# The products of the five lower decay levels: one product of a whole chunk against four quarter products

## The chip, the cores and the metric

The kernel runs on one core of one Trainium2 chip. The metric is the device time of one execution in microseconds (us); the median of three runs before is 3709.82 us (3709.05 to 3710.29).

## The reference, cut to what matters

The program is a stack of one block (a hybrid mixer and a mixture of experts) and two layers of a second block. The second block has four mixing branches. Two of them, the HGRN-2 branch and the gated linear attention (GLA) branch, decay their state by channel: within a chunk the score of query t and key s is a sum over channels d in which each channel has its own decay.

```python
cum = jnp.cumsum(fc, axis=-2)
rel = jnp.where(causal, cum[..., :, None, :] - cum[..., None, :, :], -jnp.inf)
scores = jnp.einsum('bhtd,bhsd,bhtsd->bhts', qc, kc, jnp.exp(rel))
o = jnp.einsum('bhts,bhsv->bhtv', scores, vc) + jnp.einsum('bhtd,bhdv->bhtv', qc * jnp.exp(cum), state)
```

## The kernel before, in words

The 1024 tokens are taken as 8 chunks of 128. A "unit" is a head, or a pair of heads. Each of the two layers runs 12 units in the order `KIND = "ssgghhhhrrrr"`: two SSM units, two GLA units (`g`, two heads of 64 channels each, which lie on partitions 0 to 63 and 64 to 127), four HGRN units (`h`, one head of 128 channels), four retention units. Only `g` and `h` decay by channel. So there are 4 units of kind `g` and 8 of kind `h` in the program.

For these the 128 by 128 square of scores of a chunk (keys down, queries across) is built by levels (`tensor_decay`, lines 1726 to 1787). Level l, of 0 to 6, has half width h = 2^l. It cuts the 128 tokens of a chunk into blocks of 2h tokens; in each block the keys are the first h tokens and the queries the last h. `vector_decays`, `scalar_decays` and `vector_factors` write for each level one tile E with both: the keys times their decay to the middle of the block stand in the first h columns of a block, the queries times theirs in the last h. TensorE multiplies the two, and VectorE's `copy_predicated` (line 1825) puts the result into the tile P of scores, under a mask `lm` that is true only where key and query lie in the same block (line 1822 and `constants()`). The mask drops everything else that a product has computed, or left from earlier, in its bank of PSUM.

In levels 0 to 4 the kernel before issues one product for each chunk and head: its fixed operand (the weights that are loaded into the array) is the whole chunk, 128 columns, and its moving operand is all 64 query columns of the level. In levels 5 and 6 it issues one product for each block (two of 32 columns fixed and 32 moving; one of 64 and 64). The operands are f32. In the trace each f32 product has two weight loads and two matmuls.

The order of the work is written out by hand. Each engine runs the program of a unit (its "core", here `tensor_decay`, `vector_decay`, `scalar_decay`) interleaved with the preparation of the next unit (`prep`: the projections on TensorE, lines 136 to 138, in three rounded products each; the split of their weights on ScalarE line 1357 and VectorE line 1362; conv, gates and cumulative sums). `PACE` says how many steps of the preparation stand ahead of each step of the core, the same for all engines (line 3830). On VectorE the step of level l holds `copy_predicated` of level l, the differences of level l + 3 (lines 1664, 1666), the factors of level l + 2 (lines 1683, 1687), then steps of the preparation. On TensorE it is the products of the level and then projections. An `h` unit with an even number prepares an odd one, which has no projection of values, so that it has few steps of preparation; an odd one prepares an even one (or the first retention unit). After level 6 TensorE waits for the decayed keys (`kfac_last`, VectorE line 1838), which it transposes (line 1525).

Of the kernel before, what the change touches and what calls it, by code (L numbers as in the profile page):

```python
# [67 lines left out]
class Marks:  # L68
# [5 lines left out]
    def up(self, signal, *key, by=1):  # L74
        name = HOME.get(signal, signal)
        n = self.n[name] = self.n.get(name, 0) + by
        assert not self.dry or (signal,) + key not in self.place
        self.place[(signal,) + key] = n
        return self.sem.get(name), by

    def at(self, signal, *key):
        if self.dry:
            return None, 1
        return self.sem[HOME.get(signal, signal)], self.place[(signal,) + key]
# [42 lines left out]
def c8(t):  # L127
    return t.rearrange("p (c t) -> p c t", t=128)
# [31 lines left out]
def build(nc, d, out):  # L160
    ctx = ExitStack()
    with ctx:
# [43 lines left out]
        def tl(*key):  # L206
            i = wa.has[key]
            return WA[:, i * 1024:(i + 1) * 1024]
# [5 lines left out]
        def ps(*key):  # L214
            return bank_aps[banks.has[key]]

        def free(e, room, *key):
            for end in room.was[key]:
                e.wait_ge(*at(*end))
# [1081 lines left out]
        def count(U):  # L1301
            return 2 if KIND[U % 12] == "g" else 1
# [7 lines left out]
        def k_ready(U):  # L1310
            kind = KIND[U % 12]
            return ("rot", U, 1) if kind == "r" else ("copied", "k", U, 1) if kind == "g" else ("kscaled", U) if U >= 12 else ("ksig", U)

        def head_rows(U, n):

            return slice(n * 64, (n + 1) * 64) if KIND[U % 12] == "g" else slice(0, 128)
# [203 lines left out]
        def tensor_turn(t, U, src, ready):  # L1520
            t.wait_ge(*at(*ready))
            for i in range(2):
                free(t, banks, "turn", U, i)
                for j in range(4):
                    o = t.transpose(ps("turn", U, i)[:, j * 128:(j + 1) * 128], c8(src)[:, 4 * i + j, :], ident)  # L1525
                o.then_inc(*up("turn", U, i))
# [13 lines left out]
        def tensor_states(t, U):  # L1540
            t.wait_ge(*at("copied", "v", owner(U), 3))
            for i in range(2):
                free(t, banks, "kv", U, i)
                t.wait_ge(*at("turned", U, i))
                for c in range(4 * i, min(4 * i + 4, 7)):
                    for n in range(count(U)):
                        rows = head_rows(U, n)
                        o = t.matmul(ps("kv", U, i)[rows, (c % 4) * 128:(c % 4) * 128 + 128], c8(tl("KE", U))[:, c, rows], val(U, n, c),  # L1548
                                     start=True, stop=True)
                o.then_inc(*up("kv_mm", U, i))  # L1550
# [21 lines left out]
        def tensor_outputs(t, U, n, qd, masked):  # L1572
            P, s, rows = tl("P", U, n), tl("s", U), head_rows(U, n)
            t.wait_ge(*at(*masked(1)))
            for i in range(2):
                free(t, banks, "o", U, n, i)
                for j in range(4):
                    c = 4 * i + j
                    t.matmul(ps("o", U, n, i)[:, j * 128:(j + 1) * 128], val(U, n, c), c8(P)[:, c, :], start=j == 0, stop=False)  # L1579
            for i in range(2):  # L1580
                t.wait_ge(*at("state", U, 3 + 3 * i))
                for j in range(4):
                    c = 4 * i + j
                    if c:
                        o = t.matmul(ps("o", U, n, i)[:, j * 128:(j + 1) * 128], c8(s)[rows, c, :], c8(qd)[rows, c, :], start=False,  # L1585
                                     stop=j == 3)
                o.then_inc(*up("o_mm", U, n, i))
# [13 lines left out]
        def tensor_norm(t, U, n):  # L1601
            for i in range(2):
                free(t, banks, "om", U, n, i)
                t.wait_ge(*at("osq", U, n, i))
                t.matmul(ps("om", U, n, i), ones, half(tl("osq", U, n), i), start=True, stop=True).then_inc(*up("om_mm", U, n, i))  # L1605
# [126 lines left out]
        def tensor_decay(t, U):  # L1732
            N = range(count(U))
            q, k = tl("q", U), tl("k", U)
            t.wait_ge(*at("copied", "q", U, 1))
            t.wait_ge(*at(*k_ready(U)))
            for i in range(2):
                for n in N:
                    free(t, banks, "base", U, n, i)
                for j in range(4):  # L1740
                    c = 4 * i + j
                    for n in N:
                        rows = head_rows(U, n)
                        o = t.matmul(ps("base", U, n, i)[:, j * 128:(j + 1) * 128], c8(k)[rows, c, :], c8(q)[rows, c, :],  # L1744
                                     start=True, stop=True)
                        if j == 3:
                            o.then_inc(*up("scores", U, n, i))

            def products(l):
                h = 1 << l  # L1750
                E = tl("E", U, l)
                t.wait_ge(*at("fac", U, l))
                for n in N:
                    free(t, banks, "pd", U, l, n)
                for c in range(8):
                    for n in N:
                        rows = head_rows(U, n)
                        chunk = c8(E)[rows, c, :]
                        if l < 5:
                            second = chunk.rearrange("p (j b) -> p j b", b=2 * h)[:, :, h:2 * h]  # L1760
                            o = t.matmul(ps("pd", U, l, n)[:, c * 64:(c + 1) * 64].rearrange("p (j r) -> p j r", r=h),  # L1761
                                         chunk if l else c8(k)[rows, c, :], second, start=True, stop=True)
                        for b in range(0, 128 if l >= 5 else 0, 2 * h):
                            o = t.matmul(ps("pd", U, l, n)[b:b + h, c * 64 + b // 2:c * 64 + b // 2 + h], chunk[:, b:b + h],
                                         chunk[:, b + h:b + 2 * h], start=True, stop=True)
                        if c == 7:
                            o.then_inc(*up("prod", U, l, n))

            for l in range(6):
                yield  # L1770
                products(l)
            yield
            products(6)
            tensor_turn(t, U, tl("F", U), ("kfac_last", U))
            yield
            tensor_states(t, U)
            yield
            t.wait_ge(*at("qfac_last", U))
            for n in N:
                tensor_outputs(t, U, n, tl("E", U, 7), lambda i: ("placed", U, 6, n))  # L1780
                yield
                tensor_norm(t, U, n)
# [2643 lines left out]
```

## Time and profile before

| | before |
|---|---|
| median of 3 runs | 3709.82 us |
| the profiled execution | 3709.18 us, of which the span from first to last instruction is 3707.4 us |
| PE busy | 3526.8 us (95%) |
| DVE busy | 1964.9 us (53%) |
| ACT busy | 1572.8 us (42%) |
| mean granted TensorE clock | 0.976 |

PE is TensorE's matmul row, PEld its weight loads, DVE VectorE, ACT ScalarE. A busy PE counts each matmul from its start to its modelled end, and matmuls overlap, so a busy share says little on how dense the work is; the starts in a timeline do. A granted clock of 1.00 is 2.4 GHz, 0.50 is 1.2 GHz. The levels lie in two parts of the span: 1811 to 2222 us (layer 0: units 2 and 3 of kind `g`, then 4 to 7 of kind `h`) and 2895 to 3320 us (layer 1, units 14 to 19).

### The profile page before, as it was taken

The numbers are of one execution on the slowest core, as the hardware profiler recorded it, in microseconds if no ns is written. First come the engines' busy times: TensorE is split into PE (matmuls) and PEld (weight loads), VectorE is DVE, ScalarE is ACT, GpSimd is POOL, SyncE is SP. The second block draws the span as 40 slices with busy tenths as digits, with TensorE's granted clock in tenths as the row PEclk, the third lists the DMA queues.
The fourth block names the chain that finished last, engine by engine and source line by source line (L and its number), as shares of the span: only waits on it lengthen the run. The fifth ranks groups of instructions, "written<-read, shape, count | busy, mean of one in ns | idle before, by whom it ended". The sixth has DMA issues, their size and how long they took to land.

```text
span 3707.4 us, 45567 instructions
## 1 busy us (share of the span) xinstructions
PE 3526.8 (95%) x18870; PEld 2833.7 (76%) x18870; DVE 1964.9 (53%) x2556; ACT 1572.8 (42%) x1826; POOL 90.9 (2%) x90
## 2 busy tenths in 40 slices
PE   7999999989999997999999999999999999999998
PEld 5787667766666664778887888787778887888777
DVE  4544443465555554655555563445565556663434
ACT  4322101355545552543346454434443456653433
POOL 0000000000000002000000000000000000000000
PEclk9999999989999998999999999999999999999999
DMA  5101342369999996122111011243122101011332
GB/s 199 46 26 52 125 155 90 127 248 369 370 367 373 367 366 254 64 69 80 46 46 58 21 66 58 76 179 128 61 74 69 46 36 52 35 58 46 126 130 102
DMA packets 95876, 487.55 MB, mean 132 GB/s; under 512 B 10752, under 2 KB 11264, under 8 KB 57776
## 3 DMA queue, kind: packets, MB, share of 16 engines
q1 hardware_dynamic: 77216, 417.31, 30.6%
q0 software_dynamic: 12688, 46.27, 3.4%
q10 hardware_dynamic: 5760, 20.97, 1.4%
q8 instruction: 153, 2.51, 0.3%
q14 instruction: 59, 0.48, 0.0%
HBM read 427.23 MB, written 57.28 MB: 131 GB/s over the span
## 4 chain that ended last, share of the span: by engine, by line
PE 50%; ACT 4%; DVE 4%; issue 2%; DMA 0%; DVEq 0%; ACTq 0%; POOLq 0%
PE ps L136 13%; PE ps L138 13%; PE ps L137 13%; PE ps L1761 2%; PE ps L1605 1%; PE ps L1585 1%; PE ps L1579 1%; PE ps L1548 1%; PE ps L1744 1%; PE ps L3521 1%; PE ps L1525 1%; PE ps L3527 0%; PE ps L374 0%; PE ps L278 0%; PE ps L382 0%
## 5 line engine op out<-in xcount | busy, mean ns | idle before, releaser
L136 PE MATMUL ps<-HH,WS 128*128 128x512 f32 (+1 forms) x2608 | 1047.4, 402 | 30.3 <-DVE WS L1362 22.4
L138 PE MATMUL ps<-HH,WS 128*128 128x512 f32 (+1 forms) x2608 | 1024.0, 393 | 0.0
L137 PE MATMUL ps<-HL,WS 128*128 128x512 f32 (+1 forms) x1968 | 773.6, 393 | 0.0
L136 PEld LDWEIGHTS ps<-HH,WS 128*128 128x128 f32 (+1 forms) x2608 | 494.6, 190 | 147.2 <-DVE WS L1362 26.4
L138 PEld LDWEIGHTS ps<-HH,WS 128*128 128x128 f32 (+1 forms) x2608 | 492.9, 189 | 107.8
L1425 ACT ACTIVATE WA<-ps 128x512 f32<-128x512 f32 x240 | 142.9, 596 | 813.3 <-PE ps L138 744.3
L137 PEld LDWEIGHTS ps<-HL,WS 128*128 128x128 f32 (+1 forms) x1968 | 374.0, 190 | 76.0 <-issue 1.5
L1362 DVE TENSOR_TENSOR WS<-RAW,WS 128x1024 fp32r<-128x1024 f32 (+1 forms) x153 | 200.6, 1312 | 175.4 <-ACT WS L1357 175.3
L136 PE MATMUL ps<-WS,HH 128*128 128x256 f32 x896 | 262.4, 293 | 12.6 <-DVE HL L2238 12.2
L137 PE MATMUL ps<-WS,HH 128*128 128x256 f32 x896 | 255.5, 285 | 0.0
L138 PE MATMUL ps<-WS,HL 128*128 128x256 f32 x896 | 255.4, 285 | 0.0
L720 DVE TENSOR_TENSOR WRR<-WR,WAR 128x2048 fp32r<-128x2048 f32 x72 | 162.7, 2288 | 138.1 <-ACT WAR L716 138.1
L136 PE MATMUL ps<-WAR 128*128 128x512 f32 x512 | 212.9, 416 | 3.6 <-DVE WAR L1181 3.6
L138 PE MATMUL ps<-WAR 128*128 128x512 f32 x512 | 201.3, 393 | 0.0
L137 PE MATMUL ps<-HH,WS 128*128 128x512 f32 x512 | 199.9, 391 | 0.0
L136 PEld LDWEIGHTS ps<-WS,HH 128*128 128x128 f32 x896 | 174.0, 194 | 21.1 <-issue 13.4
L1825 DVE COPY_PREDICATED WA<-LM,ps 128x512 f32<-128x512 int32 x112 | 97.0, 900 | 167.0 <-PE ps L1761 138.8
L1357 ACT ACTIVATE WS<-RAW 128x1024 fp32r<-128x1024 f32 (+1 forms) x153 | 171.5, 1122 | 24.9 <-PE ps L138 13.7
L137 PEld LDWEIGHTS ps<-WS,HH 128*128 128x128 f32 x896 | 174.1, 194 | 2.0 <-issue 2.0
L138 PEld LDWEIGHTS ps<-WS,HL 128*128 128x128 f32 x896 | 173.9, 194 | 0.0
L716 ACT ACTIVATE WAR<-WR 128x2048 fp32r<-128x2048 f32 x72 | 135.0, 1910 | 72.0 <-PE ps L138 70.2
L4061 DVE TENSOR_TENSOR WS<-RAW,WS 128x1024 fp32r<-128x1024 f32 x64 | 78.3, 1224 | 148.4 <-ACT WS L4053 148.4
(406 smaller groups left out, 5294.5 us busy)
## 6 DMA issues: line engine op xcount, KB each, us to landing
WR<-in_weu SPq DMA_DIRECT2D x37, 1024.0 KB, 6.9
WR<-in_weg SPq DMA_DIRECT2D x35, 1024.0 KB, 8.4
WR<-in_wed SPq DMA_DIRECT2D x34, 1024.0 KB, 9.6
RAW<-in_wo SPq DMA_DIRECT2D x32, 1024.0 KB, 4.8
H<-in_wed SPq DMA_DIRECT2D x26, 1024.0 KB
WA<-in_wada SPq DMA_DIRECT2D x48, 512.0 KB, 4.7
H<-in_weg SPq DMA_DIRECT2D x23, 1024.0 KB
H<-in_weu SPq DMA_DIRECT2D x21, 1024.0 KB
```

Of the source, the lines that this page charges most:

```text
L136: t.matmul(o, l[0], r[0], start=st, stop=False)
L137: t.matmul(o, l[0], r[1], start=False, stop=False)
L138: return t.matmul(o, l[1], r[0], start=False, stop=sp)
L716: a.activation(rounded(j, p), raw_piece("wg", j, p), ACT.Copy).then_inc(*up("we_hi", j, p))
L720: v.tensor_tensor(rest_of(j, p), raw_piece("wg", j, p), rounded(j, p).bitcast(F32), ALU.subtract).then_inc(*up("we_lo", j, p))
L1357: a.activation(parts(layer, n)[0], raw_of(layer, n), ACT.Copy).then_inc(*up("w_hi", layer, n))
L1362: v.tensor_tensor(lo, raw_of(layer, n), hi.bitcast(F32), ALU.subtract).then_inc(*up("w_lo", layer, n))
L1425: a.activation(half(tl(*dst), i), ps("pj", layer, n, i), func, scale=scale).then_inc(*up("copied", *dst, i))
L1525: o = t.transpose(ps("turn", U, i)[:, j * 128:(j + 1) * 128], c8(src)[:, 4 * i + j, :], ident)
L1761: o = t.matmul(ps("pd", U, l, n)[:, c * 64:(c + 1) * 64].rearrange("p (j r) -> p j r", r=h), chunk if l else c8(k)[rows, c, :], second, st ...
L1825: v.copy_predicated(pv, mv, bv).then_inc(*up("placed", U, l, n))
L4061: v.tensor_tensor(lo, wo_raw(layer, i, k), hi.bitcast(F32), ALU.subtract).then_inc(*up("wo_lo", layer, i, k))
```

## The change

Levels 0 to 4 now issue four products for each chunk and head instead of one. Product b of the four takes as fixed operand the 32 columns b to b + 31 of the chunk, as moving operand the 16 query columns of the level among the same 32 tokens, and writes PSUM partitions b to b + 31 and 16 columns. The four squares of 32 tokens on the diagonal hold all blocks of these levels. Levels 5 and 6 come out of the same loop as before. The rest of the kernel is unchanged.

```diff
-                        if l < 5:
-                            second = chunk.rearrange("p (j b) -> p j b", b=2 * h)[:, :, h:2 * h]
-                            o = t.matmul(ps("pd", U, l, n)[:, c * 64:(c + 1) * 64].rearrange("p (j r) -> p j r", r=h),
-                                         chunk if l else c8(k)[rows, c, :], second, start=True, stop=True)
-                        for b in range(0, 128 if l >= 5 else 0, 2 * h):
-                            o = t.matmul(ps("pd", U, l, n)[b:b + h, c * 64 + b // 2:c * 64 + b // 2 + h], chunk[:, b:b + h],
-                                         chunk[:, b + h:b + 2 * h], start=True, stop=True)
+                        keys = chunk if l else c8(k)[rows, c, :]
+                        size, m = max(2 * h, 32), max(h, 32)
+                        for b in range(0, 128, size):
+                            second = chunk[:, b:b + size].rearrange("p (j b) -> p j b", b=2 * h)[:, :, h:2 * h]
+                            to = ps("pd", U, l, n)[b:b + m, c * 64 + b // 2:c * 64 + (b + size) // 2]
+                            o = t.matmul(to.rearrange("p (j r) -> p j r", r=h), keys[:, b:b + m], second, start=True, stop=True)
```

## Rows read from the trace of the kernel before

**Rows 1.** The page, part 1: busy us, share of the span, instructions.
```profile
PE 3526.8 (95%) x18870; PEld 2833.7 (76%) x18870; DVE 1964.9 (53%) x2556; ACT 1572.8 (42%) x1826; POOL 90.9 (2%) x90
```

**Rows 2.** Busy time by stretch, units 2, 3, 5, 7: the heading names the columns.
```profile
core 0: us, PE busy (x) PEld busy (x) DVE busy (x) ACT busy (x) POOL busy (x), PEclk, DMA share, GB/s
1811.00:1858.00 47.00, 47.00 (x458) 41.17 (x457) 32.86 (x40) 16.89 (x20) 0.00 (x0) 1.00 0.12 46
1902.00:1949.00 47.00, 47.00 (x479) 42.27 (x478) 32.75 (x43) 15.57 (x19) 0.00 (x0) 1.00 0.06 23
2046.00:2091.00 45.00, 45.00 (x350) 41.45 (x349) 25.64 (x34) 15.55 (x19) 0.00 (x0) 1.00 0.03 13
2177.00:2222.00 45.00, 45.00 (x350) 41.52 (x348) 26.28 (x34) 14.96 (x21) 0.00 (x0) 1.00 0.03 13
```

**Rows 3.** Instructions of line 1761 and who waits for them.
```profile
L1761 PE MATMUL ps<-WA x1280: 217/272/322, 1811.3 to 3306.5; 64*128 64x64 f32 x92, 128*128 128x64 f32 x91
```

**Rows 4.** Timeline of PE, level 1 of unit 5: start us, us, instruction.
```profile
2053.65 0.28 PE L138 MATMUL ps<-WS,HL 128*128 128x256 f32 x1
2053.77 1.90 PE L1761 MATMUL ps<-WA 128*128 128x64 f32 x16
...
2055.67 0.28 PE L137 MATMUL ps<-WS,HH 128*128 128x256 f32 x1
```

**Rows 5.** Timeline of PE, level 1 of unit 2.
```profile
1818.97 0.28 PE L138 MATMUL ps<-WS,HL 128*128 128x256 f32 x1
1819.18 2.00 PE L1761 MATMUL ps<-WA 64*128 64x64 f32 x32
...
1821.34 0.28 PE L137 MATMUL ps<-WS,HH 128*128 128x256 f32 x1
```

**Rows 6.** Timeline of PE, level 5 of unit 5.
```profile
2083.13 0.39 PE L138 MATMUL ps<-HH,WS 128*128 128x512 f32 x1
2083.45 0.70 PE L1764 MATMUL ps<-WA 128*32 128x32 f32 x32
2084.08 0.50 PE L136 MATMUL ps<-HH,WS 128*128 128x512 f32 x1
2084.42 0.39 PE L137 MATMUL ps<-HL,WS 128*128 128x512 f32 x1
2084.65 0.40 PE L138 MATMUL ps<-HH,WS 128*128 128x512 f32 x1
```

**Rows 7.** Timeline of PE, level 5 of unit 2.
```profile
1849.54 0.39 PE L138 MATMUL ps<-HH,WS 128*128 128x512 f32 x1
1849.86 0.76 PE L1764 MATMUL ps<-WA 64*32 64x32 f32 x64
...
1850.88 0.40 PE L137 MATMUL ps<-HL,WS 128*128 128x512 f32 x1
```

**Rows 8.** Busy time of the stretch in which the records of level 5 start.
```profile
1849.85:1850.43 0.58, 0.58 (x65) 0.57 (x64) 0.00 (x0) 0.40 (x1) 0.00 (x0) 1.00 0.00 0
```

**Rows 9.** Timeline of PE, level 6 of unit 5.
```profile
2089.75 1.15 PE L1764 MATMUL ps<-WA 128*64 128x64 f32 x16
2090.82 0.66 PE L1525 MATMUL ps<-CT,WA 128*128 128x128 f32 x4
```

**Rows 10.** Timeline of DVE: the copies of levels 0 or 1 in units 2, 3, 5.
```profile
1821.22 2.50 DVE L1825 COPY_PREDICATED WA<-LM,ps 128x512 f32<-128x512 int32 x2 [0.68 <-PE ps L1761]
1904.51 2.49 DVE L1825 COPY_PREDICATED WA<-LM,ps 128x512 f32<-128x512 int32 x2 [3.89 <-PE ps L1761]
2048.16 1.32 DVE L1825 COPY_PREDICATED WA<-LM,ps 128x512 f32<-128x512 int32 x1 [4.39 <-PE ps L1761]
```

**Rows 11.** Unit 6: DVE, ACT and PE where each was last kept waiting.
```profile
2124.05 1.32 DVE L1825 COPY_PREDICATED WA<-LM,ps 128x512 f32<-128x512 int32 x1 [4.12 <-PE ps L1761]
2136.84 1.06 ACT L1674 ACTIVATE WA<-WA 128x1024 f32<-128x1024 f32 x1 [1.94 <-DVE WA L1666]
2154.56 1.23 DVE L1838 TENSOR_TENSOR WA<-WA 128x1024 f32<-128x1024 f32 x1 [1.20 <-ACT WA L1792]
2155.84 0.88 PE L1525 MATMUL ps<-CT,WA 128*128 128x128 f32 x6 [0.87 <-DVE WA L1838]
```

**Rows 12.** Unit 6: busy time by stretch, DVE in the first, ACT in the second.
```profile
2124.10:2139.10 15.00, 15.00 (x87) 13.08 (x86) 14.90 (x20) 4.97 (x5) 0.00 (x0) 1.00 0.09 36
2136.90:2155.60 18.70, 18.07 (x136) 15.31 (x134) 12.45 (x16) 18.50 (x19) 0.00 (x0) 1.00 0.24 85
```

**Rows 13.** Waits of PE in unit 16, in all.
```profile
PE ps L1525 <- DVE WA L1838: 6.4, 1, 6.4
PE ps L136 <- DVE WS L1362: 1.5, 2, 1.1
```

**Rows 14.** Unit 4: the wait at its end, and the clock behind it.
```profile
2023.88 1.59 PE L1525 MATMUL ps<-CT,WA 128*128 128x128 f32 x8 [1.76 <-DVE WA L1838]
2024.00:2028.00 4.00, 4.00 (x15) 3.42 (x16) 3.97 (x4) 3.96 (x4) 0.00 (x0) 0.57 0.00 0
```

## The prediction
> **What bounds the kernel now.** I read the page's busy shares first, then busy time by stretch for the units that the change touches, then timelines of PE around single levels, and last the timelines of DVE and ACT for who waits for whom. PE is busy 95% of the span against 53% for DVE and 42% for ACT [rows 1]. In units 2, 3, 5 and 7 it never stops: 47.00 of 47.00 us, 45.00 of 45.00, with DVE at 33 or 26 and ACT at 15 to 17 [rows 2]. So there the time of a level is read from the starts on PE, and what PE gets rid of the unit gets rid of, as long as DVE follows. Units 4, 6, 16 and 18 are another matter (below).
>
> The line that changes has 1280 matmuls [rows 3]. That is 8 `h` units and 4 `g` units of two heads, so (8 + 8) heads of 5 levels of 8 chunks = 640 products, with two records each. By levels: 8 x 5 = 40 levels of `h`, 4 x 5 = 20 of `g`.
>
> **The change part by part.** It has one part, on PE. To price a level with all that it disturbs, I take the start of the last projection matmul before it, the start of the second one behind it, and subtract the two steps that would lie between them without a level: 0.12 us each where the projection moves 256 columns, 0.23 each where it moves 512 (2084.65 - 2084.42) [rows 6].
>
> - `h`, levels 0 to 4 before: 2055.67 - 2053.65 - 0.24 = 1.78 us for 16 records [rows 4].
> - `g`, levels 0 to 4 before: 2.37 - 0.24 = 2.13 us for 32 records [rows 5].
> - `h`, level 5, 32 records of 32 columns fixed: 2084.42 - 2083.13 - 0.46 = 0.83 us [rows 6].
> - `g`, level 5, 64 records of 32 columns fixed: 1850.88 - 1849.54 - 0.46 = 0.88 us [rows 7]. Its 64 weight loads lie within 0.58 us [rows 8], 9 ns a record; the other 0.31 us is paid on going in and out.
>
> Behind the change a level of `h` has 4 x 16 = 64 records and one of `g` 128, all with 32 columns fixed and 16 moving. The trace has no product that uses four strips of 32 columns of the array on all 128 rows. The bounds: from above, that products of a chunk which read the same 128 rows don't overlap; then a record costs half of one with 64 columns. Those of level 6 take (2090.82 - 2089.75) / 16 = 67 ns with the way out, some 58 without it [rows 9], so 29 ns each, 64 x 0.029 + 0.31 = 2.17 us, 0.39 more than now. From below, the 9 ns a record of level 5 of `g`, where four products run side by side (two heads, two strips). Between them is level 5 of `h`: two strips on the same 128 rows, 32 records in about 0.50 us (0.63 to the next start less 0.13), 16 ns. A record of 64 columns costs 58 ns and one of 32 columns 16: that is half for the width and half again because two strips work at once. So strips on the same rows do overlap, by two. I take it that they overlap by four: then 64 records of `h` stand as those 64 of level 5 of `g` do, at 9 ns. The new level of `h` costs 0.88 us, and **0.90 us goes** (with two strips at a time 64 x 0.016 + 0.31 = 1.33, and 0.45 goes).
>
> For `g` eight products could run side by side, but I don't take a gain from that: 9 ns a record is then about the pace at which PE is fed. 128 records are twice the 0.57 us, and with 0.31 us that is 1.45 us; **0.68 us goes**. If eight did run side by side, the level would fall towards 0.9 us.
>
> The Trainium skill (TensorE: Matmul & The Clock Gate, Part 1, "Wait — 56ns, not 53.3ns?") speaks against the change: start to start never falls below about 25 ns however small the matmul. In this trace it isn't so for level 5, with 64 records in 0.58 us. Read as 25 ns for each f32 product of two records it is nearer, since the trace has about 18; whether 18 holds for 64 products in a row instead of 32 no row shows. It is a rival below.
>
> More instructions (1920 more products) have to be fetched; by rows the engine isn't held up for that anywhere in these stretches, and I cost it at nothing. The moving operand's stride is that of before. DVE's copy reads the same 512 columns under the same mask.
>
> What follows behind PE. A `g` unit: DVE waits 0.68 us for PE at the tightest level of unit 2, 3.89 at the first of unit 3 [rows 10]. A level shorter by 0.68 just uses up the first; the factors that PE reads are made over a level ahead, so PE doesn't feel it. All five levels count: 4 units x 5 x 0.68 = 13.6 us. Odd `h` units (5, 7, 17, 19): DVE waits 4.39 us for PE [rows 10] and is busy 26 of 45 us [rows 2]; all count: 4 x 5 x 0.90 = 18.0 us.
>
> Even `h` units (4, 6, 16, 18) have few projections between levels, and DVE and ACT set their end. In unit 6 DVE waits for PE at the copy of level 0 (2124.05), then is busy 14.90 of 15.00 us; ACT waits for it at 2136.84 and is busy 18.50 of 18.70 us; then DVE line 1838 waits for ACT, and PE for that, 0.87 us [rows 11, 12]. Only level 0 stands ahead of this chain. Units 4 and 16 show the same with 1.76 and 6.4 us [rows 13, 14]. What levels 1 to 4 save turns into wait: 4 units x 0.90 = 3.6 us count, 14.4 don't.
>
> That wait has a price. PE idle at the end of unit 4 was followed by a granted clock of 0.57 over 4 us [rows 14], that is nearly all at the lower level, 1.2 GHz, at which a stretch does half its work. With up to 3.6 us more idle in each of four units I expect one or two such stretches more, at about 1.7 us each where PE is the bound; I charge 1.5 us.
>
> Sum: 13.6 + 18.0 + 3.6 - 1.5 = 33.7 us. From the profiled execution's 3709.18 us (0.6 below the median of the three runs, which is no difference) this gives 3675.5 us.
>
> **The rivals.**
> 1. *Two strips at a time.* `h` saves 0.45 us a level, `g` as forecast: 13.6 + 9.0 + 1.8 - 1 = 23.4, so 3686 us. For it: no row has four strips. Against: two heads by two strips already make four products at once.
> 2. *PE is fed more slowly once a queue of ready products is used up.* At 25 ns a product, `h` costs 32 x 0.025 + 0.31 = 1.11 (saves 0.67), `g` 1.91 (saves 0.22): 4.4 + 13.4 + 2.7 - 1 = 19.5, 3690 us. The page's rule read by product gives the same. Read by matmul record, as it is written, it would give 1.91 and 3.5 us for a level and some 3740 us; the 9 ns in level 5 excludes that there.
> 3. *More than that.* Eight products at once in `g` (1.2 us saved a level, 24 in all), or the even units passing on more than level 0: 14.4 at most. With half of the two, 3656 us.
> 4. *Slower: no overlap of strips on the same 128 rows.* 29 ns a record; `h` loses 0.39 us a level on the 20 levels of odd units and on 4 of the even ones, 9.4 us, and `g`, where two heads still overlap, costs 128 x 0.0145 + 0.31 = 2.17, which is 0.8 us lost in all: 3719 us. It decides from a pace of 23 ns a record for `h` upward (1.78 - 0.31 = 1.47 over 64). Against it stands the 16 ns of level 5 of `h`. A change of tile shape inside a level that drains the array would have the same effect, but all products of a new level have one shape.
> 5. *The gain is nothing, since other engines bound these units.* [rows 2] speaks against it.
>
> **How the numbers follow.** Within 0.2% (7.4 us) nothing can be told from no change here. Forecast, 3668 to 3682 us: 0.55. Rivals 1 and 2 and what lies between: 0.23. Rival 3: 0.12. Rival 5 and small gains: 0.04. Rival 4: 0.06. For 8 in 10 the range takes in the forecast, rivals 1 and 2 and the near part of 3: 3662 to 3692 us. Faster by over 0.2%: 0.90; within 0.2%: 0.04; slower: 0.06.
>
> **What would show it.** In the timeline of unit 5, level 1: the level's 64 records stand between two projection matmuls about 1.1 us apart, where 2.0 were, and DVE's wait of 4.39 us in front of line 1825 falls by about 0.9. In a `g` unit a level costs 1.45 us, with 128 records. The stretches of units 5 and 7 are shorter by 4.5 us, units 2 and 3 by 3.4, units 4 and 6 by 0.9, with PE's waits in front of lines 136 and 1525 grown by 3.6 us in each. Rival 1 would show as 16 ns a record in `h` and 9 in `g`; rival 2 as a pace that breaks in the middle of a level of `g`; rival 4 as 29 ns. It would be wrong if a record's cost depends on its moving columns or on a switch of strip in a way that level 5 doesn't show, or if the idle time in the even units brings the clock down in the units behind them too.

## The result, and the profile after

| | before | after |
|---|---|---|
| median | 3709.44 us (4 runs, 3702.33 to 3710.29) | 3669.88 us (4 runs, 3669.00 to 3671.14) |
| ratio to before | | 0.9898, 95% interval 0.9881 to 0.9915 |
| span of the profiled execution | 3707.4 us | 3667.2 us |
| PE busy | 3526.8 us | 3478.5 us |

The change makes the kernel 39.6 us faster. The forecast was 33.9 us under the median, 3675.5 us. In the code after, the products of all levels are line 1764 (levels 0 to 4 were line 1761 before), the copy is line 1824 (1825 before) and the decayed keys are line 1837 (1838 before). A record is one matmul of the trace; an f32 product has two.

One level of an odd `h` unit, level 1 of unit 5, in PE's timeline (start us, us, instruction):

```profile
2041.29 0.28 PE L138 MATMUL ps<-WS,HL 128*128 128x256 f32 x1
2041.50 0.74 PE L1764 MATMUL ps<-WA 128*32 128x16 f32 x64
...
2042.38 0.28 PE L137 MATMUL ps<-WS,HH 128*128 128x256 f32 x1
```

By the reading of [rows 4]: 2042.38 - 2041.29 - 0.24 = 0.85 us, where 1.78 were. 0.93 us is gone; the forecast was 0.90. The same for `g`, level 1 of unit 2:

```profile
1815.47 0.28 PE L138 MATMUL ps<-WS,HL 128*128 128x256 f32 x1
1815.68 1.26 PE L1764 MATMUL ps<-WA 64*32 64x16 f32 x128
...
1817.10 0.28 PE L137 MATMUL ps<-WS,HH 128*128 128x256 f32 x1
```

1.63 - 0.24 = 1.39 us, where 2.13 were [rows 5]: 0.74 us gone, forecast 0.68. The pace inside this level is read from stretches that all begin at 1815.65 and end later and later; the second column of counts (PEld) is weight loads begun until then:

```profile
1815.65:1815.80 0.15, 0.15 (x23) 0.12 (x29) 0.15 (x2) 0.00 (x0) 0.00 (x0) 1.00 0.00 0
1815.65:1815.95 0.30, 0.30 (x35) 0.27 (x35) 0.30 (x2) 0.10 (x1) 0.00 (x0) 1.00 0.00 0
1815.65:1816.10 0.45, 0.45 (x50) 0.42 (x52) 0.45 (x2) 0.25 (x1) 0.00 (x0) 1.00 0.00 0
1815.65:1816.40 0.75, 0.75 (x86) 0.72 (x88) 0.75 (x2) 0.55 (x2) 0.00 (x0) 1.00 0.10 22
1815.65:1816.70 1.05, 1.05 (x122) 1.02 (x124) 1.05 (x2) 0.85 (x2) 0.00 (x0) 1.00 0.14 43
```

The first 0.12 us hold 29 loads, some 4 ns each; in the next 0.15 us only 6 begin. From 1816.10 on it is 36 in 0.30 us, 8.3 ns a record and 16.7 ns a product, twice over. The burst is followed by a halt that takes its gain back: the 52 loads until 1816.10 took 0.42 us, 8.1 ns each. Over the whole level the pace is 8.3 ns a record.

Not every level of `g` is like this one. Level 0 of unit 3 in the same profile:

```profile
1896.06 1.26 PE L1764 MATMUL ps<-WA 64*32 64x16 f32 x128
1897.70 0.38 PE L136 MATMUL ps<-WS,HH 128*128 128x256 f32 x1 [0.37 <-issue]
```

It costs 1.83 us and not 1.39: behind the 128 matmuls PE stands still for 0.37 us and waits for nothing that the profile shows.

Where the span went, by units, each from the first product of level 0 to the transpose behind level 6 (line 1525 in both), after minus before in us, worked out from PE's starts:

| | g 2, 3 | h 4 | h 5 | h 6 | h 7 | g 14, 15 | h 16 | h 17 | h 18 | h 19 | all |
|---|---|---|---|---|---|---|---|---|---|---|---|
| forecast | -3.4 each | -0.9 | -4.5 | -0.9 | -4.5 | -3.4 each | -0.9 | -4.5 | -0.9 | -4.5 | -35.2 |
| after | -3.65, -3.25 | -1.17 | -4.73 | -1.15 | -4.73 | -3.67, -3.40 | -1.17 | -4.74 | -1.13 | -4.73 | -37.5 |

The other 2.7 us of the 40.2 by which the profiled spans differ lie outside these units. The first level starts at 1808.55 us, 2.75 us earlier than before, ahead of all that the change touches; what moves there is looked at below.

The stretches of units 5 and 6:

```profile
2034.90:2074.70 39.80, 39.80 (x585) 35.48 (x584) 25.48 (x33) 15.34 (x18) 0.00 (x0) 1.00 0.04 15
2106.20:2138.70 32.50, 29.35 (x465) 23.50 (x464) 25.32 (x34) 22.09 (x23) 0.00 (x0) 0.95 0.18 66
```

In unit 5 PE still never stops, and DVE's wait in front of the copy of level 0 went from 4.39 us [rows 10] to 3.33. In unit 6 PE is now idle for 3.2 of 32.5 us, where it had waited for 0.87 [rows 11]. Here are PE's waits in unit 6, then in unit 16, to be held against [rows 13]:

```profile
PE ps L136 <- DVE WS L1362: 3.0, 2, 2.4
```
```profile
PE ps L1525 <- DVE WA L1837: 6.2, 1, 6.2
PE ps L136 <- DVE WS L1362: 3.2, 1, 3.2
```

The wait for line 1362 (the weights' split on DVE) has doubled in unit 16 (3.2 us for 1.5) and is new in unit 6 (3.0 us; before, PE waited there for line 1838 alone). That is one part of where levels 1 to 4 of the even units went. The other is the granted clock (the column behind POOL). Unit 4 from its first product to its transpose, before and after:

```profile
1987.48:2023.88 36.40, 33.14 (x226) 28.51 (x224) 27.91 (x37) 22.13 (x23) 0.00 (x0) 1.00 0.19 73
```
```profile
1977.91:2013.13 35.22, 30.30 (x466) 24.24 (x465) 27.98 (x37) 22.12 (x23) 0.00 (x0) 0.90 0.20 76
```

Five levels of 0.93 us are 4.65 us less work on PE. The unit is 1.2 us shorter and PE's idle time in it has grown from 3.3 to 4.9 us. The remaining 1.8 us are PE's own work taking longer. A mean clock of 0.90 over 35.2 us is, by estimate, 7 us at the lower level, in which work could lose up to 3.5 us; part of the 7 us is idle time. In unit 16 the clock went from 0.95 to 0.88, in unit 6 from 1.00 to 0.95, in unit 18 from 0.97 to 0.94.

### The profile page after: what moved, and what is told of

Its sections match the earlier page's. It is cut to its first block, busy times and chain, and to the rows that moved or that the text cites. A ratio compares the mean times of both kernels' runs of the same rounds, so it can differ in the third digit from the quotient of the medians.

```text
span 3667.2 us, 53247 instructions
## 1 busy us (share of the span) xinstructions
PE 3478.5 (95%) x22710; PEld 2777.2 (76%) x22710; DVE 1963.7 (54%) x2556; ACT 1572.9 (43%) x1826; POOL 91.4 (2%) x90
## 4 chain that ended last, share of the span: by engine, by line
PE 49%; ACT 5%; DVE 4%; issue 2%; DMA 0%; DVEq 0%; ACTq 0%; POOLq 0%
PE ps L136 13%; PE ps L138 13%; PE ps L137 13%; PE ps L1764 1%; PE ps L1605 1%; PE ps L1585 1%; PE ps L1579 1%; PE ps L1548 1%; PE ps L1744 1%; PE ps L3520 1%; PE ps L3526 0%; PE ps L374 0%; DVE WS L1362 0%; PE ps L1525 0%; ACT L1425 0%
```

## The experiments

**Each kind of unit alone.** The width of a level's products is put under a name:

```diff
-                        size, m = max(2 * h, 32), max(h, 32)
+                        W = 32 if l >= 5 or count(U) == 1 else 128      # h only
+                        W = 32 if l >= 5 or count(U) == 2 else 128      # g only
+                        size, m = max(2 * h, W), max(h, W)
```

> Four quarter products only in the 8 h units; the 4 g units keep one product a chunk. Theory (the time of a level on PE is what counts, in even h units only level 0 and what the trace of after shows beyond it): the stretches of the h units became shorter by 1.8, 4.6, 1.1, 4.7 us in layer 0 and 1.7, 4.7, 0.8, 4.7 us in layer 1 when both kinds were changed, 24.0 us in all, so 3709.4 - 24 = 3685 us. Rival (the gain needs both kinds, or lies outside the units, as 2.5 us before the first level in the profile of after): 3680 us or less, or 3690 us or more.

Measured: 3686.18 us (ratio 0.9937, 0.9921 to 0.9954), 23.4 us faster. The units' own sum is 23.5: -1.17, -4.74, -1.14, -4.73 in layer 0 and, within 0.01 us, the same in layer 1, and 0.00 in all four `g` units.

> Four quarter products only in the 4 g units. Theory: 20 levels of 2.13 us became levels of 1.39 us, 0.74 us each, of which the profile of after shows 3.7, 3.2, 3.7, 3.2 us by unit, 13.8 us: 3695.6 us. The sum of the gains of this kernel and of the one with h alone is that of after, 39.6 us less what lies outside the units (up to 2.5 us). Rival (something else moved too): the two gains add up to under 34 or over 42 us.

Measured: 3688.74 us (ratio 0.9950, 0.9933 to 0.9967), 20.8 us faster, 7 more than expected. By units it is -3.63, -3.65, -3.38, -3.59, 14.3 us in all, as expected; its profile shows the first level at 1805.45 us, 5.85 us earlier than before, ahead of everything that the kernel changes; in the profile of the kernel with `h` alone it is at 1817.74 us, 6.4 later. The sum of the two gains is 44 us, outside the expected 34 to 42, so the rival's condition (something else moved too) is met; the sum of the two kernels' units is 37.8 against 37.5 of both together. So the units add up, and the medians of these kernels carry up to some 7 us that belong to something else.

**Is that something else a property of a kernel?** The changed kernel and the kernel before were each run and profiled a second time.

> The changed kernel once more, beside the others. Theory: 3670 us, g units shorter than before by 3.65 us, odd h units by 4.85, even ones by 1.4, each within 0.3 us; what lies ahead of the first level differs from the profile of after by up to some us, since this part moved by 12 us from kernel to kernel in which its instructions are the same. Rival (the part ahead belongs to the change): again 2.8 us earlier than before at the first level.

> The kernel before once more, one look. Theory: the start of the first level lies some us off 1811.3 us although nothing is changed; the units themselves are as long as in the first profile within 0.3 us. Rival (the part ahead is steady for one and the same kernel): within 0.5 us of 1811.3.

Measured: the changed kernel again 3668.02 us, units -3.65, -3.39, -1.15, -4.70, -1.14, -4.70 and so on, 37.8 in all, first level at 1807.50 us, 3.8 earlier than in the first profile of before. The kernel before, one execution, 3700.99 us: all twelve units within 0.01 us of their lengths in the first profile, but the first level at 1804.38 us, 6.9 earlier:

```profile
1804.38 0.33 PE L1761 MATMUL ps<-WA 64*128 64x64 f32 x2
```

Nothing is changed there, so an early first level is no mark of the change. The first levels of all ten profiles lie between 1804.38 and 1817.74 us. Part of it can be seen in one stretch, 90 to 130 us, in the first profile of the kernel before and then in the second (the column behind POOL is the granted clock):

```profile
90.00:130.00 40.00, 37.83 (x170) 29.80 (x169) 23.95 (x39) 16.86 (x20) 0.00 (x0) 0.87 0.08 27
```
```profile
90.00:130.00 40.00, 37.81 (x187) 30.41 (x186) 23.71 (x38) 18.24 (x22) 0.00 (x0) 0.96 0.07 27
```

With the clock at 0.96 instead of 0.87 of full, 17 more matmuls fit in. Held against each other matmul by matmul, the two profiles of before show that most of the 6.9 us arises in a few steps. The second profile's lead grows from 1.1 to 4.4 us at 110 to 124 us, where the granted clock is 0.61 in the first profile (111 to 124 us) and 0.83 in the second (110 to 120). It falls back by 1.3 us at 163 to 175 us, where the first has the higher clock (0.86 against 0.76), and reaches 7.0 us at 298 us. From 124 to 164 us, with a clock of 1.00 in both, it doesn't move. So up to 300 us the difference goes with the clock, in both directions; how it moves between 4.1 and 8.1 us from there to the first level was not followed.

**The even `h` units.** Levels 1 to 4 of units 4, 6, 16 and 18 go back to one product a chunk:

```diff
+                        W = 32 if l >= 5 or l == 0 or count(U) == 2 or U % 2 else 128
```

> As after, but the even h units (4, 6, 16, 18) take four quarter products in level 0 alone; their levels 1 to 4 are one product a chunk again, 16 levels of 0.93 us more on PE. Theory (DVE and ACT set the end of these units): little comes back, the 5.2 us these units gained in all less 4 x 0.9 = at most 1.6 us: 3670 to 3672 us. Rival (PE's time counts there as in the odd units): 16 x 0.93 = 14.9 us, 3685 us.

Measured: 3671.80 us (ratio 0.9900, 0.9883 to 0.9916), 1.9 above after, which is less than what medians carry from outside the units. The even units are 1.16, 1.07, 1.15, 1.07 us shorter than before, against 1.17, 1.15, 1.17, 1.13 with all levels changed. So 14.9 us of PE's time were put back and 0.2 us came of it. In unit 6 of this kernel PE has no wait for line 1362, where after has 3.0 us; its wait at the unit's end is 0.81 us, as it was before the change (0.87), and the granted clock in units 4 and 6 is 1.00 again. That PE's time in levels 1 to 4 doesn't set the end of these units is shown by this. That DVE and ACT do is read from who waits for whom [rows 11, 12]; no run made them faster or slower. Level 0 alone brings 1.07 to 1.16 us a unit and not the 0.93 of its own cost; the rest wasn't traced.

**The order of the strips.** The same products, with the loop over the strip outside that over the chunks:

```diff
-                for c in range(8):
-                    for n in N:
-                        ...
-                        for b in range(0, 128, size):
+                for b in range(0, 128, size):
+                    for c in range(8):
+                        for n in N:
+                            ...
```

> As after, with the same quarter products in another order: all chunks' first strips, then all second strips, and so on, so that products that follow each other use the same 32 columns of the array (in g units the two heads still alternate). Theory (the gain is that neighbouring products work in different strips at once): 29 ns a record in h, 14.5 in g; a level costs 64 x 0.029 + 0.31 = 2.17 us in h and 2.17 in g, more than the 1.78 and 2.13 of before: 3709.4 + 24 x 0.39 + 0.8 = 3719 to 3722 us. Rival (a product of 32 fixed and 16 moving columns is cheap by itself, at some 9 ns a record, in any order): 3670 us.

Measured: 3710.03 us (ratio 1.0001, 0.9992 to 1.0011): the whole gain is gone, but it isn't the 3719 to 3722 us that was expected. Level 1 of unit 5 in its timeline:

```profile
2058.21 0.28 PE L138 MATMUL ps<-WS,HL 128*128 128x256 f32 x1
2058.42 1.90 PE L1766 MATMUL ps<-WA 128*32 128x16 f32 x64
2060.24 0.39 PE L136 MATMUL ps<-WS,HH 128*128 128x256 f32 x1
2060.47 0.28 PE L137 MATMUL ps<-WS,HH 128*128 128x256 f32 x1
```

2060.47 - 2058.21 - 0.24 = 2.02 us, where the same 64 records, taking turns from strip to strip, take 0.85. That is (2.02 - 0.31) / 64 = 27 ns a record, not the 29 of the expectation; in `g` 2.04 us a level, some 14 ns a record (128 records). By units: odd `h` +1.09, `g` -0.40, even `h` 0 to +0.17, +3.0 in all, where 10.2 was expected: 4.3 us in the odd `h` units for 7.8, 0.3 in the even ones for 1.6, and in `g` a gain of 1.6 for a loss of 0.8, since the records cost 27 and 14 ns for 29 and 14.5 and the even units passed little on. A quarter product is cheap only because its neighbours work in other strips. By itself it costs what its fixed width costs: 27 ns a record with 32 columns, 58 with 64 [rows 9], some 1.78 / 16 = 111 with 128 [rows 4].

**Two products of half a chunk.** 64 fixed and 32 moving columns:

```diff
+                        W = 32 if l >= 5 else 64                        # both kinds
+                        W = 64 if l < 5 and count(U) == 2 else 32       # g only, h as after
```

> Levels 0 to 4 in both kinds of unit as two products a chunk and head with 64 fixed and 32 moving columns, instead of four with 32 and 16. Theory (a product costs its width, 58 ns a record at 64 columns, divided by the strips that work at once, unless PE is fed more slowly, at 16.7 ns a product): h: 32 records, two at once, 29 ns each, a level 0.93 + 0.31 = 1.24 us instead of 0.86; g: 64 records, four at once, 14.5 ns each, 0.93 + 0.31 = 1.24 instead of 1.39. In units: odd h 5 x 0.54 = 2.7 us gained over before, even h 0.9, g 5 x 0.89 = 4.4: 32 us in all, 3677 us. Rival (narrower is better in both, g is at its strips' limit and not at the feed's): a g level costs 1.4 us or more.

Measured: 3670.87 us (ratio 0.9901, 0.9885 to 0.9918), against 3706.37 us of the kernel before beside it: 35.5 us faster, 6 us lower than the 3677 expected. By units: `g` -4.37 each, odd `h` -2.78, even `h` -0.77, 31.7 in all, as expected; the rest lies outside them. In `h` two half products are worse than four quarters (odd units -2.78 for -4.73), in `g` they are better.

> g units as two products of 64 fixed and 32 moving columns, h units as the four quarter products of after. Theory (g in after is bound by how fast products are fed, not by the array): a g level costs 1.24 us instead of 1.39, 20 x 0.15 = 3 us under after: 3667 us, if the parts outside the units stay as they are. Rival (no better than after, or lost in the waits behind the levels): 3670 us or more, with g units 3.65 us shorter than before or less.

Measured: 3665.27 us (3664.64 to 3666.16; ratio 0.9889, 0.9872 to 0.9905), against 3668.02 us (3666.69 to 3671.61) of the changed kernel beside it: 2.8 us better. That is less than what medians carry from outside the units, so the units decide: `g` -4.37, -4.36, -4.37, -4.36, `h` as after, 41.0 in all, 3.2 to 3.5 more than the two profiles of the changed kernel. A level of `g`:

```profile
1817.02 0.28 PE L138 MATMUL ps<-WS,HL 128*128 128x256 f32 x1
1817.23 1.14 PE L1765 MATMUL ps<-WA 64*64 64x32 f32 x64
...
1818.51 0.28 PE L137 MATMUL ps<-WS,HH 128*128 128x256 f32 x1
```

1.49 - 0.24 = 1.25 us, with 64 records of twice the width, where 128 narrow ones take 1.39. Here the narrow ones don't pay: eight could run side by side, and they come at 16.7 ns a product all the same. With 27 ns a record in one strip, eight at once would allow 3.4 ns a record, by estimate; they run at 8.3. And no level of `g` in this kernel shows the halt without a wait that level 0 of unit 3 shows above.

## Why the prediction was right

**Which units count, and PE in them.** Right. In `g` and odd `h` units PE's saving is the unit's saving: 5 x 0.93 = 4.65 for 4.73 measured, 5 x 0.74 = 3.70 for 3.25 to 3.67. What unit 3 lacks is in its level 0 (1.83 us for 1.39), with the 0.37 us in which PE waits for nothing that the profile shows. I had costed the fetching of 1920 more products at nothing, since no row of before showed a halt for it. In all four profiles in which the 128 records of a `g` level come at 8.3 ns, one or two such levels are 0.2 to 0.45 us longer than the others; none is with half the records (`g` as half products) or with 128 records at 14 ns (strip after strip). So that term wasn't nothing, though under 1 us in all; that it is the fetching is argued, not shown. The tight place of [rows 10] (DVE 0.68 us ahead in unit 2) cost nothing.

**The price of an `h` level.** Right, and it was the choice that carried most. The trace had two strips on the same rows [rows 6] and two heads by two strips [rows 7]; that four strips on the same rows overlap was taken, not seen. The runs show it from both sides: 0.85 us with neighbours in other strips, 2.02 with the same products in the other order. The slower rival's mechanism exists, then, and its price was near (27 ns a record for 29), which was not enough for the 3719 us that I had put to it; what decides is the order of the products, and the change's order is the right one. Rival 1 (two strips at a time, 16 ns a record, 1.33 us a level) is refuted by 0.85.

**The price of a `g` level.** Right in mechanism: 1.39 us for 1.45. I had said that 9 ns a record was about the pace at which PE is fed. It is 8.3 ns; 128 of them are 1.06 us instead of my 1.14, and that is the difference. The burst of some 30 records at 4 ns at the start gains nothing, since PE halts behind it. Rival 2 (25 ns a product in a long row) didn't come: 64 products in a row keep 16.7 ns. The rule that I had quoted from the Trainium skill (TensorE: Matmul & The Clock Gate, Part 1), some 25 ns from start to start at the least, doesn't hold here for records or for products whose neighbours are in other strips. Products that follow each other in one strip take 27 ns a record, which the rule would allow.

**The even `h` units.** Right that little but level 0 counts; 1.15 us a unit for 0.90. The sum of the four was 4.6 us for 3.6. What I had said of the sign of it was too simple: PE's waits were to grow by 3.6 us in each unit, and PE's idle time grew by 1.5 to 2.3 us in units 4, 6 and 16 and by 3.9 in unit 18. In the first three the rest of the saved time went into work at a lower clock.

**The charge for the clock.** Wrong as a cost, 1.5 us, though right in that the clock falls. It fell inside the even units (unit 4 from 1.00 to 0.90), where PE isn't the bound: with the clock back at 1.00 in units 4 and 6 in the run of level 0 alone these units ended no earlier. And behind unit 4, where I had read a price off [rows 14], the clock rose: from 0.92 before to 1.00 over the 22 us to unit 5, and that stretch became 0.6 us shorter. Behind units 16 and 18 it changed by less (0.87 to 0.91, 0.90 to 0.88), and the odd units kept 1.00.

**Sum.** 37.5 us in the units for 35.2 forecast, 2.3 us of sizes; the charge of 1.5 us didn't come; and some 2 us are what moves in the rest of the program. The forecast's errors all lie on one side, so none hid another. The last of them it couldn't have priced: the start of the first level alone moves by more than that from execution to execution. In rival 3 the 3656 us are a slip: half of what it gains over the forecast, (24 - 13.6 + 14.4) / 2 = 12.4 us, gives 3663 us.

## What to carry to other kernels

Small f32 products that write different strips of 32 PSUM partitions run side by side even when they read the same 128 rows, so cutting a product to its useful squares pays (0.85 us a level for 1.78), if products that follow each other go to different strips; the same products strip after strip gained nothing. Stop cutting when the product costs less than PE can be fed (16.7 ns for an f32 product here): in `g` units, with eight strips, half as many of twice the width were better; in `h` units, with four, they were not. And look for the unit's own bound first: in the four units where, by the waits, DVE and ACT set the end, 15 us of PE's time bought 0.2.

## What the runs showed of the hardware that was not expected

- The f32 products of a level of `g` enter PE in a burst, a halt and a steady run: 29 weight loads in 0.12 us, 6 in the next 0.15 us, later 36 in each 0.30 us. On average the start is no faster than the rest. What makes the burst and the halt was not tried.
- PE stood still for 0.37 us behind 128 short matmuls without a wait in the profile. The cause is open.
- One and the same kernel started its first level at 1811.3 and at 1804.4 us in two profiles, with all twelve units the same within 0.01 us; up to 300 us the steps between them stand where the granted clock differs. Differences of a few us between medians of different kernels are better read from the stretches that the change touches.
